# The second half of the chunk states moved back in VectorE's order, in a two-block kernel on one Trainium2 core

## What is computed

```
h = _rms(x, norm1_w) * (1 + sc1) + sh1
u, q, k, v = split(h @ w_in)                       # 512, 512, 128, 128 columns
# S5: 32 groups of 16 inputs and 64 complex states, over 512 steps
bu = einsum(u, bb);   s = scan(a * s_before + bu)  # complex
y = s_re @ c_re - s_im @ c_im + d_skip * u
z = gelu(y);          y_ssm = z * sigmoid(z @ w_glu + b_glu)
# attention: 8 query heads, 2 key/value heads, window of 128, blocks of 128
q, k = _rms(q, q_norm_w), _rms(k, k_norm_w)        # per head of 64
logits = q @ k_band.T / 8 + bias;  m = max(rowmax(logits), sink)
p = exp(logits - m);  y_attn = p / (sum(p) + exp(sink - m)) @ v_band
x = x + g1 * (concat(_rms(y_ssm), _rms(y_attn)) @ w_out)
```

## Time and profile before

| | before |
|---|---|
| median of 3 runs | 1930.44 us (1930.17 to 1930.57) |
| the profiled execution | 1928.16 us |
| its span | 1926.5 us |
| busy: PE, DVE, ACT, POOL | 1828.4, 1030.0, 718.7, 161.8 us |
| the second mixer's stretch with the change | about 1376 to 1433 us from the start of the span |

### The profile page before, as it was taken

How to read it: one execution, slowest core, us unless ns; L and a number is a source line. 1 busy time by engine, 2 the same in 40 slices (tenths; PEclk the granted TensorE clock), 3 DMA queues, 4 the chain that set the end, 5 groups by cost and what they waited for, 6 DMA issues and landing times.

```text
span 1926.5 us, 23418 instructions
## 1 busy us (share of the span) xinstructions
PE 1828.4 (95%) x8801; PEld 1455.9 (76%) x8801; DVE 1030.0 (53%) x1436; ACT 718.7 (37%) x1005; POOL 161.8 (8%) x218
## 2 busy tenths in 40 slices
PE   7399999999999999999999999999878999999998
PEld 5288888886888677787788778888765778888887
DVE  4355633635555556654878733335655565555433
ACT  3122222223334686622323222223237254555322
POOL 2112100201000000003411020100000300000000
PEclk9699999999999999999999999999989999999999
DMA  7655522233222112122555452334120222222222
GB/s 202 195 174 174 174 91 73 94 106 122 88 88 88 66 45 66 66 88 89 184 170 163 132 162 68 99 108 175 39 116 23 66 81 93 87 95 90 74 91 86
DMA packets 171451, 206.77 MB, mean 107 GB/s; under 512 B 18140, under 2 KB 149786, under 8 KB 170866
## 3 DMA queue, kind: packets, MB, share of 16 engines
q1 hardware_dynamic: 144994, 161.97, 25.5%
q0 software_dynamic: 12400, 38.55, 6.4%
q10 hardware_dynamic: 13984, 5.27, 1.2%
HBM read 190.29 MB, written 17.56 MB: 108 GB/s over the span
## 4 chain that ended last, share of the span: by engine, by line
PE 91%; DVE 3%; DMA 3%; ACT 2%; issue 1%; POOL 0%; DVEq 0%; POOLq 0%; ACTq 0%
PE bank L1813 40%; PE bank L1777 34%; PE bank L2028 6%; DMA mod_raw<-in_w_mod 3%; PE bank L1745 2%; PE bank L1935 1%; PE bank L2052 1%; PE bank L1792 1%; PE bank L2063 0%; DVE w_lo L1074 0%; PE bank L2185 0%; PE bank L1833 0%; PE bank L1864 0%; PE bank L2131 0%; PE bank L2217 0%
## 5 line engine op out<-in xcount | busy, mean ns | idle before, releaser
L638 ACT CAST w_hi<-w_raw 128x2048 fp32r<-128x2048 f32 x158 | 301.2, 1907 | 874.4 <-PE bank L1813 446.2
L1074 DVE TENSOR_TENSOR w_lo<-w_raw,w_hi 128x2048 fp32r<-128x2048 f32 x157 | 370.4, 2359 | 463.6 <-ACT w_hi L638 463.4
L1813 PE MATMUL bank<-h_hi,w_hi 128*128 128x512 f32 x1088 | 436.2, 401 | 13.9 <-ACT h_hi L662 8.9
L1813 PE MATMUL bank<-h_hi,w_lo 128*128 128x512 f32 x1088 | 433.0, 398 | 0.0
L1813 PE MATMUL bank<-h_lo,w_hi 128*128 128x512 f32 x1088 | 344.5, 398 | 0.0
L1813 PEld LDWEIGHTS bank<-h_hi,w_hi 128*128 128x128 f32 x1088 | 206.4, 190 | 66.6 <-issue 17.3
L1813 PEld LDWEIGHTS bank<-h_lo,w_hi 128*128 128x128 f32 x1088 | 205.9, 189 | 50.2 <-DVE h_lo L1100 0.4
L1813 PEld LDWEIGHTS bank<-h_hi,w_lo 128*128 128x128 f32 x1088 | 206.9, 190 | 48.6 <-issue 0.2
L1777 PE MATMUL bank<-hid_hi,w_hi 128*128 128x512 f32 x528 | 208.9, 396 | 0.0
L1777 PE MATMUL bank<-hid_lo,w_hi 128*128 128x512 f32 x528 | 208.9, 396 | 0.0
L1777 PE MATMUL bank<-hid_hi,w_lo 128*128 128x512 f32 x528 | 208.9, 396 | 0.0
(11 more groups left out here) (405 smaller groups left out, 2360.2 us busy)
## 6 DMA issues: line engine op xcount, KB each, us to landing
w_raw<-in_w_in SPq DMA_DIRECT2D x29, 1024.0 KB, 5.2
mod_raw<-in_w_mod POOLq DMA_DIRECT2D x96, 256.0 KB, 3.5
w_raw<-in_ffn_w_gate SPq DMA_DIRECT2D x22, 1024.0 KB, 6.4
w_raw<-in_ffn_w_up SPq DMA_DIRECT2D x22, 1024.0 KB, 5.4
w_raw<-in_w_up SPq DMA_DIRECT2D x22, 1024.0 KB, 5.0
w_raw<-in_ffn_w_down SPq DMA_DIRECT2D x16, 768.0 KB, 4.2
w_raw<-in_ffn_w_down SPq DMA_DIRECT2D x16, 640.0 KB, 3.9
w_raw<-in_w_out SPq DMA_DIRECT2D x8, 1024.0 KB, 4.8
```

Of the source, the lines that this page charges most:

```text
L638: act.copy(w_hi[i % 2][:], w_raw[i % 2][:]).then_inc(S("w_hi_done"), 1)
L1074: dve.tensor_tensor(w_lo[s][:], w_raw[s][:], w_hi[s][:].bitcast(F32), ALU.subtract).then_inc(S("w_split"), 1)
L1813: mm = pe.matmul(bank[:], w[:, k, at], h[:, k, :], start=k == first and part == 0 and i == 0, stop=k == last and part == 1)
```

## The change

The call `chunks(1)` on DVE is moved from behind `split(n + 2)` to behind `sw_max(1)`, ahead of the loop that begins with `sw_scale(0)`. Nothing else is edited. The lines between the two places carry numbers smaller by one in the new file.

```diff
--- before.py
+++ after.py
@@ -1625,7 +1625,6 @@
             chunks(0)
             n = PART["q2"][0]
             split(n + 2)
-            chunks(1)
 
             q_v = q2_raw[:].rearrange("p b (h d) -> p (b h) d", d=QK)
             k_v = k2_raw[:].rearrange("p b (h d) -> p (b h) d", d=QK)
@@ -1686,6 +1685,7 @@
 
             sw_max(0)
             sw_max(1)
+            chunks(1)
             for u in range(0, 8, 2):
                 sw_scale(u)
                 sw_scale(u + 1)
```

## The result

The changed kernel is slower by what can just be told apart: a median of 1934.62 us against 1929.64 us for the kernel before, 18 runs of each, ratio 1.0026 with a 95% interval of 1.0019 to 1.0034. That is +5.0 us; the forecast was +5.2 us. As a time the forecast was 1935.6 us, 1.0 above the measured median; 0.8 of that is its starting point, 1930.44 us from three runs where 18 runs give 1929.64. (One execution of the changed kernel took 2543 us, at a mean granted clock of 0.67 against 0.97 in the others; it is not in the ratio and doesn't move the median.) The profiled execution took 1936.15 us.

The account below looks back on a forecast made before the run. TensorE holds 91% of the chain, but DVE bounds part of the second mixer. Front -5.3, block +11.23, covered wait and rounding -0.8 make +5.2 us; from the median 1930.44 that forecasts 1935.6 us, range 1931.8 to 1938.8.

Parts of the forecast that it names:

- DVE bounds the stretch though it is 53% busy: Second mixer, 1376 to 1441 us: DVE is the bound for a while; TensorE idles 7.62 us for the normed queries.
- The front, 5.3 us gained: Norms through key tile copies: last copy ends at 1399.45 instead of 1404.72, limited by TensorE's products and ScalarE's queue.
- tiles three to six: Query and key tiles turned by TensorE and copied by ScalarE: 1.05 + 0.9 + 0.95 + 0.95 from 1394.9.
- The block, 11.23 us, paid whole: Second half of the chunk states, now behind the first maxima: its 11.23 us delay unit 0's scaling, ending at 1415.6.
- The exponentials covered, -0.8: DVE's 0.81 us wait for ScalarE's exponentials before unit 1's turning: the states now cover it.
- +5.2 at the turning of unit 1: TensorE's turning of unit 1 starts at 1417.9 instead of 1412.67, and the delay goes through whole.
- Clock 0, between -5.1 and +2.0: TensorE's granted clock over the mixer: net effect taken as 0, with gains and losses bounded on either side.
- four effects that I had bounded: TensorE's clock: query transposes gain 1.7, later low stretch at most 3.4; one more scores block loses 0.9, values 1.1 us.
- The clock pays it back: Rival: query transposes and the later low stretch return up to 1.7 and 3.4 us, giving 1930.5; chance 0.26.
- The front gives nothing: Rival: something other than DVE holds the query transposes, so +10.4 us, 1940.9; chance 0.10.
- Transposes do not raise the clock: Rival: low level lasts over first values and most of the next scores, +6.8 us, 1937.2; chance 0.06.
- Queues: SP's loads behind DVE's splits come some 3 us earlier, ready before TensorE wants them; worth nothing either way.

Follow-up runs that it names:

- e3: The changed kernel with `chunks(1)` moved behind the scaling of units 0 and 1 on DVE; 1928.70 us, ratio 0.9995.
- e10: The changed kernel with `chunks(1)` behind the scaling of units 0 and 1, chunk outputs 0 and 1 copied before the maxima of units 2 and 3; 1925.14 us.
- e6: The kernel before, with 7.3 of the 11.2 us of the states' second half left out, block in its old place; 1924.13 us, ratio 0.9976.
- e7: The changed kernel, with 7.3 of the 11.2 us of the states' second half left out, block in its new place; 1927.80 us, ratio 0.9992.
- e2: The changed kernel with `chunks(1)` moved ahead of the maxima of units 0 and 1; 1934.05 us, ratio 1.0023.
- e5: The changed kernel with `chunks(1)` moved between the query norms and the key reduction on DVE; 1930.85 us, ratio 1.0013.
- e4: The changed kernel with TensorE's chunk products of quarters 0 and 1 (7.1 us) moved ahead of the turning of unit 0; 1930.88 us, ratio 1.0006.
- e9: The changed kernel with 17 unused products added on TensorE between scores 1 and the turning of unit 0; 1932.88 us, ratio 1.0017.
- e8: The changed kernel with 12 unused products added on TensorE between scores 1 and the turning of unit 0; 1934.28 us, ratio 1.0027.
- e11: The changed kernel with states behind the scaling, early copies of chunk outputs 0 and 1, and TensorE's first-half chunk products before unit 0's turning; 1921.97 us, ratio 0.9955.

## Why the prediction was right, point by point

- *DVE bounds the stretch though it is 53% busy.* Right: e3 and e10, which differ from the change in DVE's order alone, win back 6.6 and 10.5 us at the norm (5.0 and 10.3 at the turning of unit 2), and e6 and e7 give 5.0 and 7.1 us for 7.3 us of DVE's work.
- *The front, 5.3 us gained.* 4.55 measured. TensorE's end of the key and value products and then ScalarE's queue are the limits, as said, and DVE had time to spare. The term that was mis-sized is that of tiles three to six, "1.05 + 0.9 + 0.95 + 0.95": 3.85 us, and 4.91 measured (1396.74 to 1401.65), from a start 0.25 us earlier than forecast. (With the last copy the terms as written end at 1399.33 and not at 1399.45, a slip of 0.1.) I took the query tiles at the low level, where they had been, and the key tiles at the 0.95 us of before, which was a duration at the high level. It came out the other way round. The clock stayed high through the query tiles (1.03 and 1.15 us for two) and fell in 1398, so that the two key tiles took 3.48 us; before they had taken 1.99. The prediction let the clock only win in front ("1.7 us more gained"); it lost 0.7.
- *The block, 11.23 us, paid whole.* Right: 11.23 us long at the new place, and from scores 0 to the turning of unit 0 the shift grows by 11.25 (-4.55 to +6.70).
- *The exponentials covered, -0.8.* Right: the wait is gone, and e2 brought it back as 0.80.
- *+5.2 at the turning of unit 1.* With the front 0.7 short that makes +5.9; +5.8 at the scores behind it.
- *Clock 0, between -5.1 and +2.0.* Of the four effects that I had bounded two came, smaller: +0.7 (values 0, out of at most 1.1) and -1.3 (the later low stretch, out of at most 3.4). The scores after values 0 weren't low, and the gain in front came as the loss of 0.7 above. Together that is +0.1, so 5.3, and +5.26 at the norm. The 0 that I took for the clock was right by luck: three shifts of 0.7 to 1.3 us cancelled. "The clock pays it back" had the right mechanism for 1.3 of its 5.1 us, and the wrong sign for its front part.
- *The front gives nothing.* Excluded by scores 0 at -4.55. e5, whose block stands ahead of the key reduction, shows what that case looks like.
- *Transposes do not raise the clock* (the rival that the Trainium skill, TensorE: Matmul & The Clock Gate, part 4, PE-mode transpose, stands for). A part of its price came, the first values low (1.90 us). But the scores after them were high (1.13 us at 1425.44), and the +6.8 did not come. On the rule itself the rows disagree: before, the clock rose after 3.7 us of nothing but transposes, and in e5 it was still low, 0.50 in the window of 1405, though from 1400.14 to 1405.7 TensorE had turned query and key tiles without a gap (the key tiles as ordinary products by the identity). That stays open; no run was made for it alone.
- *Queues.* Nothing of SP's loads shows in any wait of the stretch.

## What to carry to other kernels

When a block is moved out of one engine's way, ask twice: what becomes the limit at the place it leaves (here the gain was 4.6 of 11.2 us), and what the waiting engine could do at the place it goes to. The same block behind the scaling instead of ahead of it, where TensorE has some 13 us of products that need none of its results (values 0 need the bank that its first four products read), was worth 6.6 us at the norm, 1.6 of them through the clock; with the first outputs' copies ahead of the next maxima as well (e10), 10.5. And a filler moved into a pause uncovers what it covered before: e4 won 2.8 us, and with the next wait removed as well, 6.9.

## What was unexpected of the hardware

- TensorE's clock fell behind pauses of 1 to 3 us, and not in them, but when TensorE was at work again. In e9 it fell at 1419, after 14.9 us of products, idle times of just 1.18 and 0.35 us and two blocks of transposes of 0.66 us. In the change it stayed high through an idle 2.94 us and fell in 1398, during the transposes. Transposes aren't needed for it: 17 us earlier the change has a pause of 2.52 us among the key and value products, which both kernels share, and the clock fell 0.9 us behind it, within products that followed each other without a gap:

```profile
1379.91 0.38 PE L1777 MATMUL bank<-w_hi,h_hi 128*128 128x256 f32 x1 [2.52 <-DVE w_lo L1074]
```

```profile
1380.00:1381.00 1.00, 1.00 (x8) 0.91 0.03 11
1381.00:1382.00 1.00, 1.00 (x7) 0.50 0.76 248
```

- In longer pauses it fell at very different points: 1.2 us after TensorE had stopped in the change's pause of 15.97 us, 3.9 in e8 and 4.5 in the kernel before (1390.8 to 1395.4). And the two pauses around the turning of unit 2 (2.33 and 0.45 us) brought a low stretch in the change and none in e3 and e11. No run here separates what decides on it.
- At the low level a pair of key tiles (16 products of 128x64 by the identity, x32) took 3.48 us, and at the high level 1.99 before; such a short stretch of low clock costs as much as a missed wait.
- From execution to execution the same code before the stretch differed by up to 3.2 us, more than half of the effect, so that only offsets inside the stretch showed the terms.
